# Combine products over three PSUM banks, with the gated rows' transposes ahead of the last two

## The reference

```python
def hier_moe(xf, w_rg, b_rg, w_re, b_re, w1, w3, w2):
    ...                      # two experts of 32 for each token, and their gates
    def expert_block(args):
        xblk, e = args
        return (jax.nn.silu(xblk @ w1[e]) * (xblk @ w3[e])) @ w2[e]

    yb = lax.map(expert_block, (xb, block_exp)).reshape(R, D)
    out = jnp.zeros((T + 1, D), yb.dtype).at[row_tok].add(yb * row_gate[:, None].astype(yb.dtype))
    return out[:T]
```

## Time and profile before

| | us |
|---|---|
| median of 3 runs | 2274.24 |
| lowest, highest | 2269.87, 2276.2 |
| profiled execution, its own time | 2264.46 |
| its span (first to last instruction) | 2262.6 |
| TensorE busy (share of the span) | 2153.8 (95%) |
| mean DMA rate over the span | 270 GB/s |

### The profile page before, as it was taken

How to read it: one execution, slowest core, us unless ns; L and a number is a source line. 1 busy time by engine, 2 the same in 40 slices (tenths; PEclk the granted TensorE clock), 3 DMA queues, 4 the chain that set the end, 5 groups by cost and what they waited for, 6 DMA issues and landing times.

```text
span 2262.6 us, 21849 instructions
## 1 busy us (share of the span) xinstructions
PE 2153.8 (95%) x8991; PEld 1129.6 (50%) x8991; DVE 882.4 (39%) x1623; ACT 314.9 (14%) x686; POOL 46.6 (2%) x62
## 2 busy tenths in 40 slices
PE   7999999998999999999899999999899899989898
PEld 4557766455577764444633333333345543333333
DVE  3336665326365654022432333323575422121122
ACT  2221001215310003000100000000134100000000
POOL 0000000000000000000100000000000000000000
PEclk9999999998999999999899999999999899999999
DMA  9347766350276675121899999999320899999995
GB/s 356 119 149 260 260 238 232 124 186 34 81 261 226 243 269 186 40 74 38 349 424 418 413 411 418 414 413 394 130 76 1 350 427 425 427 428 426 427 427 243
DMA packets 142532, 612.00 MB, mean 270 GB/s; under 512 B 15320, under 2 KB 66200, under 8 KB 117728
## 3 DMA queue, kind: packets, MB, share of 16 engines
q1 hardware_dynamic: 135328, 596.07, 66.7%
q0 software_dynamic: 7008, 14.40, 1.8%
q10 hardware_dynamic: 96, 0.10, 0.0%
HBM read 616.07 MB, written 4.33 MB: 274 GB/s over the span
## 4 chain that ended last, share of the span: by engine, by line
PE 91%; ACT 3%; DVE 3%; issue 2%; DMA 1%; SPq 0%; ACTq 0%; DVEq 0%
PE psum L2058 19%; PE psum L494 14%; PE psum L981 13%; PE psum L2078 10%; PE psum L2091 8%; PE psum L956 6%; PE psum L1559 4%; PE psum L534 3%; PE psum L2031 1%; PE psum L969 1%; PE psum L607 1%; PE psum L2068 1%; PE psum L480 1%; ACT consts L2253 1%; PE psum L1695 1%
## 5 line engine op out<-in xcount | busy, mean ns | idle before, releaser
L981 PE MATMUL psum<-normed_t,ring 128*128 128x256 f32 x1408 | 305.5, 379 | 0.0
L981 PEld LDWEIGHTS psum<-normed_t,ring 128*128 128x128 f32 x1408 | 267.5, 190 | 40.6 <-issue 4.3
L494 PE MATMUL psum<-ring,normed_t 128*128 128x512 f32 (+1 forms) x672 | 267.0, 557 | 9.9 <-DVE small L447 2.5
L886 DVE SCALAR_TENSOR_TENSOR arena<-ring,silu_c,arena 128x1024 f32<-128x1024 f32 x168 | 204.5, 1278 | 0.0
L494 PEld LDWEIGHTS psum<-ring,normed_t 128*128 128x128 f32 x672 | 124.3, 200 | 142.5 <-issue 140.9
L2078 PE MATMUL psum<-ring,consts 128*64 128x512 f32 x640 | 169.8, 594 | 21.5 <-ACT consts L2253 19.7
L2416 DVE TENSOR_TENSOR scaled<-scaled,psum 128x512 f32<-128x512 f32 x32 | 22.0, 687 | 426.8 <-PE psum L2058 426.8
L2091 PE MATMUL psum<-consts 128*128 128x512 f32 x384 | 186.1, 606 | 1.1 <-DVE small L447 0.2
L2058 PE MATMUL psum<-ring,arena 128*64 128x512 f32 x640 | 173.4, 609 | 9.7 <-issue 9.2
L2058 PE MATMUL psum<-ring,consts 128*64 128x512 f32 x640 | 168.4, 593 | 6.8 <-issue 6.8
L2411 DVE TENSOR_TENSOR resid<-resid,psum 128x512 f32<-128x512 f32 x192 | 131.8, 687 | 48.2 <-PE psum L2091 48.2
(11 more groups left out here) (398 smaller groups left out, 2217.0 us busy)
## 6 DMA issues: line engine op xcount, KB each, us to landing
ring<-in_w SPq DMA_DIRECT2D x120, 2048.0 KB, 18.0
arena<-in_w SPq DMA_DIRECT2D x48, 2048.0 KB, 19.6
ring<-in_w_mod SPq DMA_DIRECT2D x24, 2048.0 KB, 8.1
normed_t<-in_w SPq DMA_DIRECT2D x24, 2048.0 KB, 21.0
ring<-in_ffn_w_up SPq DMA_DIRECT2D x44, 1024.0 KB, 9.4
ring<-in_ffn_w_down SPq DMA_DIRECT2D x10, 2048.0 KB, 9.4
ring<-in_ab_w_in SPq DMA_DIRECT2D x6, 2048.0 KB, 17.3
ring<-in_ple_w_gate SPq DMA_DIRECT2D x4, 2048.0 KB, 9.5
```

Source lines behind the costliest of these rows:

```text
L494: m = te.eng.matmul(PS[:, bank, 0:n], src[:, k0 + k, P * t:P * t + P], w[:, k, :], start=(k == 0), stop=(k == kc - 1))
L886: ins = dv.scalar_tensor_tensor(out=acc, in0=w, scalar=sc, in1=acc, op0=ALU.mult, op1=ALU.add)
L981: m = pe.matmul(PS[:, b, 256 * hf:256 * hf + 256], w[:, hf, k, P * cc:P * cc + P], HT[:, k, 0:T], start=(k == 0), stop=(k == KC - 1))
```

## The change

`unit_bank` sends the combine products round banks 5, 0, 1 instead of 4, 5. The wait for an addition goes from the one two products back to the one three back; products 1 and 2, the first in banks 0 and 1, wait for the copies of the next pair's turned rows (`xt0`, `xt1`) out of these banks. `hidt.c` has bank 4 to itself, loses its wait for `add`, and stands ahead of the last two combine products (the sixth and seventh in MoE0, counted from 0; the second and third in MoE1). `pe_turn` gets a wait for the last addition of three pairs back. The last pair's combine, behind the loop, keeps its order and has the three banks; the layer hands over which addition frees which bank to the next one.

```diff
+                self.unit_bank = [(5, 0, 1)[i % 3] for i in range(2 * nt)]
...
                 if c >= 1:
                     pe.wait_ge(sems["act"], upto("act", f"{L}.xt0.{c - 1}"))
                     pe.wait_ge(sems["dve"], upto("dve", f"{L}.xt1.{c - 1}"))
+                if c >= 3:
+                    pe.wait_ge(sems["dve"], upto("dve", f"{L}.add{2 * self.nt - 1}.{c - 3}"))
...
                 pe.wait_ge(sems["dve"], upto("dve", f"{L}.prod.{c}"))
-                if c >= 1:
-                    pe.wait_ge(sems["dve"], upto("dve", f"{L}.add{2 * self.nt - 2}.{c - 1}"))
                 for j in range(4):
                     m = pe.transpose(PS[:, 4, P * j:P * j + P], HP[:, j::4], ident)
                 p.step(m, f"{L}.hidt.{c}")
+                if c >= 1:
+                    self.pe_combine(te, c - 1, (2 * self.nt - 2, 2 * self.nt - 1))
                 self.loaded(pe, c, 2)
                 pe.wait_ge(sems["act"], upto("act", f"{L}.hgt.{c}"))
...
-            def pe_combine(self, te, c):
+            def pe_combine(self, te, c, part):
                 pe, p, L = te.eng, te.p, self.L
                 pe.wait_ge(sems["dve"], upto("dve", f"{L}.pick.{c}"))
-                for i, (t, n) in enumerate(self.units):
+                for i in part:
+                    t, n = self.units[i]
                     pe.wait_ge(sems["dve"], upto("dve", f"{L}.{('yx', 'yc')[t // 2]}{n}.{c}"))
-                    if i >= 2:
-                        pe.wait_ge(sems["dve"], upto("dve", f"{L}.add{i - 2}.{c}"))
-                    m = pe.matmul(PS[:, 4 + i % 2, :], PICK[:, t, :], YW[t // 2][:, 512 * n:512 * n + 512], start=True, stop=True)
+                    if i >= 3:
+                        pe.wait_ge(sems["dve"], upto("dve", f"{L}.add{i - 3}.{c}"))
+                    elif i and c + 2 < PAIRS:
+                        wait(pe, *(("act", f"{L}.xt0.{c + 2}") if i == 1 else ("dve", f"{L}.xt1.{c + 2}")))
+                    m = pe.matmul(PS[:, self.unit_bank[i], :], PICK[:, t, :], YW[t // 2][:, 512 * n:512 * n + 512], start=True, stop=True)
                     p.step(m, f"{L}.sum{i}.{c}")
...
-                        self.pe_combine(te, c - 1)
+                        self.pe_combine(te, c - 1, range(2 * self.nt - 2))
...
-                self.pe_combine(te, PAIRS - 1)
-                last = 2 * self.nt - 1
-                te.banks = {4: ("dve", f"{L}.add{last - 1}.{PAIRS - 1}"), 5: ("dve", f"{L}.add{last}.{PAIRS - 1}"),
-                            6: ("dve", f"{L}.{self.free}0.{PAIRS - 1}"), 7: ("dve", f"{L}.{self.free}1.{PAIRS - 1}")}
+                self.pe_combine(te, PAIRS - 1, range(2 * self.nt))
+                te.banks = {b: ("dve", f"{L}.add{i}.{PAIRS - 1}") for i, b in enumerate(self.unit_bank)}
+                te.banks |= {6: ("dve", f"{L}.{self.free}0.{PAIRS - 1}"), 7: ("dve", f"{L}.{self.free}1.{PAIRS - 1}")}
...
-                    p.step(dv.tensor_tensor(xr, xr, PS[:, 4 + i % 2, :], ALU.add), f"{L}.add{i}.{c}", *keys)
+                    p.step(dv.tensor_tensor(xr, xr, PS[:, self.unit_bank[i], :], ALU.add), f"{L}.add{i}.{c}", *keys)
```

## The result

| | before | after |
|---|---|---|
| median, us | 2272.73 | 2244.22 |
| lowest, highest | 2269.87, 2276.2 | 2242.36, 2246.47 |
| profiled execution, its own time | 2264.46 | 2246.47 |
| its span | 2262.6 | 2244.6 |

The ratio of the times is 0.9878, 95% interval 0.9866 to 0.9890: 28 us less (28.5 by the medians), against a forecast of 2245 and 29.8 less. The two profiled executions are only 18.0 apart.

The account below looks back on a forecast made before the run. TensorE bounds MoE0's pairs until the weights' queue catches up; the queue bounds MoE1. Gains of 28.2 in MoE0 and 1.6 in MoE1 make 29.8, off 2274.24: 2244.4, say 2245 us; range 2236 to 2260.

Parts of the forecast that it names:

- Three banks: MoE0 combine products: waits for DVE's additions vanish, three steps of 0.24 us, 0.72 a pair.
- Transposes ahead of the last two: MoE0 pair: last two products cover ACT's eviction, 0.87 us, and up to 0.3 of the transposes' pipeline drain.
- New waits: Products 1 and 2 wait for ACT's and DVE's copies, pe_turn for an old addition; all hidden, costing nothing.
- Rival 3: Gap moves: products 1 and 2 wait for copies, up to 0.8 us a pair, or drain stays; 2256; chance 0.09.
- The weights catch up in MoE0: TensorE gains 0.95 us a pair on the weights' queue; its 7.7 lead at pair 3 is gone about pair 11.
- ten steps of 30.05: MoE0 weight landings from 1192.8: ten such steps and two of 29.3 put pair 15's w3 weights at 1551.9.
- Rival 1: MoE0's queue really needs TensorE's 31.1 us a pair, so only pair 3's lead is spent; 2255; chance 0.14.
- rival 2: Weights keep up throughout MoE0, at 29.1 us a pair or less; total 32.1, 2242; chance 0.08.
- MoE0's 28.2: Whole MoE0 gain in us: 25.7 up to pair 15's w3, its own 2.0, and 0.5 in the last combine.
- MoE1: Queue sets the pace, so only the layer's end gains: 1.4 us in the last pair, 0.25 in the last combine, 1.6.
- rival 4: Slower: longer MoE1 waits bring 1.2 GHz stretches of 1.7 us each that eat the gain; 2275 to 2285; chance 0.04.
- The carried 9.8: Unexplained us by which the median of runs exceeds the profiled execution, added unchanged to 2234.7 to give 2244.4.

Follow-up runs that it names:

- the second of before: The kernel before, unchanged, run once more for a second profile; that profiled execution took 2271.8 us.
- the late kernel after: Changed kernel with MoE0's pair 0 out stage moved ahead of the next pair's transposes; 2242.99 us, then 2242.73, ratio to before 0.9879.

## Why the prediction was right, point by point

- **Three banks**, put at 0.72 a pair and up to 0.1 for hidt's wait: 1.0 measured, a period of 30.07 for 31.09. The transposes' wait was a full fourth step, 0.26, which the forecast had at 0.1.
- **Transposes ahead of the last two**, put at 0.87 and up to 0.3 of drain: 0.95 measured on top of the three banks, 30.07 to 29.12. The 0.87 is right, another 0.07 is the out stage's (7.09 to 7.02), and the drain is nothing: hidt's piece goes from 0.73 to 0.47 as soon as its wait for an addition goes, in the kernel with three banks alone too.
- **Their sum**, 2.0 a pair and a period of 29.1, was met with 29.12. That the total came out has some luck in it: the drain was put at 0.3 too much, and the fourth step and the out stage at 0.2 too little.
- **New waits**, put at nothing: right. No wait of the products for ACT's or DVE's copies in the profile. Rival 3 falls.
- **The weights catch up in MoE0**: right, with a period of 30.0 and waits ahead of w3. A pair loses the 0.9 forecast, 0.69 as a wait and 0.22 in the stage behind it. It begins at pair 11 as forecast, but not as I worked it out. The execution profiled had 10.0 of lead at pair 3, not 7.7, and at pair 10 still 2.5, which steps of 30.05 would have used up only about pair 13. The step to pair 11's landing took 32.2. From pair 3's to pair 15's landing it took 362.4 where I had 359.1; two other profiles have a long step at the same pair (33.4 in the second of before, 32.1 in that of the late kernel after), for which no cause was looked for. So the term "ten steps of 30.05" was 3.3 too small. Rival 1 (31.1 a pair, whose sum is 19.3 and not the 19.5 given) and rival 2 (never binding) both fall.
- **MoE0's 28.2**: 25.2 with the layer changed alone. The 25.7 up to pair 15's w3 stage is borne out when the two profiles with a slow first pair are compared, 1586.2 in the second of before and 1560.8 after, 25.4; but these ends lie 8.6 and 8.9 later than where I had them, and the 25.7 came through because both moved together. The 2.5 that I added behind pair 15 was given back in the profile after: from there to MoE1's first silu it takes 218.7, where before takes 218.1 in both profiles. In the profile TensorE stands for 2.63 us ahead of attention's first projection (L494), where it had stood for 2.39, but here the clock is low behind it: the window 1592.5 to 1599.5 has a granted clock of 0.51, and the next 1.00. The first profile of before has 1.00 there. Such a stretch costs some 3 us. It stands in the kernel with MoE1 alone changed too, so the change in MoE0 isn't needed for it; neither profile of before has it, and what brings it is open.
- **MoE1**: 1.6 forecast, 0.3 measured with an interval that reaches to some 6 less. At its end the profile has 5.50 - 4.10 = 1.4 and 0.25 in the last four products (3.65 for 3.90), as worked out.
- **The clock** (rival 4): the waits grew from 23.3 to 35.8 and the stretches at 1.2 GHz in MoE1's pairs from five to nine, granted clock 0.98 to 0.96. The time they cost is time that TensorE had saved, and the layer is no longer than it was (434.7 for 435.4 from first silu to last). The Trainium skill's rule (TensorE: Matmul & The Clock Gate, "HAM oscillation — how this bites in real kernels"), that waits for transfers between bursts pull the clock down each time, is borne out only in part by these counts, five stretches for 13 waits before and nine for 18 after; here they cost nothing where the queue sets the pace.
- **The carried 9.8** was the one thing I could not explain, and it decides: the sum against the profiled execution gave 2234.7, and the profiled execution after took 2246.5. Carrying the difference came out right because it is a feature of most executions of both kernels: some 7 us of low clock and late gather in MoE0's first pair. I did not know that, so this was luck; had the 9.8 belonged to the kernel before alone, the same sum would have been 10 us off.

## What to carry to other kernels

Before a saving on one engine is multiplied by the number of rounds, work out what the next limit needs for a round and how much lead it has: here a queue that had been 1 us a round faster than TensorE, with 8 to 10 us of lead, let most of the saving through in one layer; in the other it had been the slower one, and let next to nothing through. A product that must wait for the addition two back loses a quarter of a microsecond each second time; look for the same wait on whatever else shares the bank. And where a profiled execution is off the median by more than the effect sought, take a second profile before trusting sums against the first.

## What the runs showed of the hardware

- Behind a stand of TensorE for a gather the clock fell in eight of ten profiles, to 1.2 GHz for 10.2 to 13.7 us. It fell behind all seven stands of 4.7 to 5.4 us, and behind one of 2.3 but not behind two of 2.2 and 2.4. Compared with a stand of 2.4 at full clock, one of 5.4 with a low clock behind it made the execution some 7 us longer, 3.0 by the stand and 3.8 by the clock.
- A stretch of 3.4 us at 1.2 GHz behind a wait for weights made a stage of 32 records take 8.78 us instead of 7.09. Nine such stretches instead of five left MoE1 at 435 us, since the queue sets the pace there.
- At 415 GB/s the queue's share of busy time was already 1.00, so the share did not tell a queue with 1 us a pair to spare from a full one at 427 GB/s; the landings did.
- Four transposes of 128x128 float32 cost 0.47 us right behind a stream of products, whether products followed them or not, and 0.73 where the first of them had to wait for an addition of VectorE.
